# The last expert of a mixture layer taken in halves: gate and up alternating, down in two column halves, and the closing norm split to match

## The reference, cut to what matters

```python
def run_block(args):
    xb, e = args
    h = jax.nn.silu(xb @ w_gate[e]) * (xb @ w_up[e])
    return h @ w_down[e]
...
    h = h + hier_moe(rms_norm_2(h, norm2_gain[l]), ...)
return rms_norm_2(h, final_gain)
```

## Time and profile before

| | us |
|---|---|
| median of 3 runs | 1339.3 (1339.16 to 1340.51) |
| span of the profiled execution, first to last instruction | 1338.3 |
| PE busy / DVE busy / ACT busy | 993.2 / 455.8 / 301.0 |
| 16 DMA engines: data moved, mean rate over the span | 464.39 MB, 347 GB/s |

### The profile page before, as it was taken

One profiled execution on the slowest core, in us unless ns is written; L12 is line 12 of the kernel. 1 busy time (PEld: TensorE's weight loads), 2 busy tenths in 40 slices (PEclk: granted clock), 3 DMA queues, 4 the chain that ended last, 5 costly groups with the idle time before them and its releaser, 6 DMA issues.

```text
span 1338.3 us, 21477 instructions
## 1 busy us (share of the span) xinstructions
PE 993.2 (74%) x9156; PEld 645.0 (48%) x9156; DVE 455.8 (34%) x1013; ACT 301.0 (22%) x644; POOL 41.8 (3%) x38
## 2 busy tenths in 40 slices
PE   9999999999999876566465756756575675657575
PEld 6997778788865443233232323423242342324242
DVE  4697786688854321111110111111011111101111
ACT  5655353647442101001000110100011000101001
POOL 0000201002120000000000000000000000000000
PEclk9999999999999998788787978878797887879787
DMA  9462455325495999999999999999999999999996
GB/s 323 161 248 73 157 189 178 109 95 193 186 417 191 390 429 428 426 429 428 428 429 429 428 428 429 428 429 429 428 428 429 428 428 429 429 428 428 429 427 259
DMA packets 63348, 464.39 MB, mean 347 GB/s; under 512 B 6922, under 2 KB 15940, under 8 KB 38596
## 3 DMA queue, kind: packets, MB, share of 16 engines
q1 hardware_dynamic: 62368, 460.80, 83.6%
q10 hardware_dynamic: 932, 2.92, 0.6%
HBM read 462.66 MB, written 1.05 MB: 346 GB/s over the span
## 4 chain that ended last, share of the span: by engine, by line
DMA 51%; PE 41%; DVE 4%; SPq 2%; issue 1%; ACT 1%; POOL 0%; POOLq 0%; DVEq 0%; ACTq 0%
DMA ring<-in_w_up 50%; PE bank L2156 16%; PE bank L2683 14%; PE bank L2110 3%; PE bank L2134 2%; PE bank L2204 1%; DVE ring_lo L1332 1%; SPq L643 1%; PE bank L2217 1%; DMA consts<-in_consts 1%; PE bank L2700 1%; DVE qk L1303 0%; DVE ring_lo L1337 0%; PE bank L2254 0%; SPq L601 0%
## 5 line engine op out<-in xcount | busy, mean ns | idle before, releaser
L2683 PE MATMUL bank<-ring,expert_area 128*32 128x256 f32 x3840 | 309.8, 493 | 230.5 <-DMA ring<-in_w_up 230.5
L2683 PEld LDWEIGHTS bank<-ring,expert_area 128*32 128x32 f32 x3840 | 146.7, 141 | 387.7 <-DMA ring<-in_w_up 251.2
L1983 DVE TENSOR_TENSOR expert_area<-expert_area,bank 128x128 f32<-128x128 f32 x64 | 24.0, 375 | 476.2 <-ACT expert_area L1224 476.2
L2700 PE MATMUL bank<-ring,consts 128*32 128x256 f32 x1952 | 118.0, 382 | 74.4 <-DVE consts L1986 74.4
L2156 PE MATMUL bank<-ring_lo,xt_hi 128*128 128x512 f32 (+3 forms) x544 | 171.8, 383 | 0.3 <-DVE xt_lo L1533 0.3
L1224 ACT ACTIVATE expert_area<-bank 128x128 f32<-128x128 f32 x64 | 17.7, 277 | 623.3 <-PE bank L2683 623.3
L2700 PEld LDWEIGHTS bank<-ring,consts 128*32 128x32 f32 x1952 | 60.5, 109 | 127.9 <-DVE consts L1986 56.9
L2156 PEld LDWEIGHTS bank<-ring_lo,xt_hi 128*128 128x128 f32 x544 | 99.0, 188 | 18.5 <-issue 1.7
L2156 PE MATMUL bank<-ring_lo,xt_lo 128*128 128x512 f32 (+2 forms) x224 | 84.9, 379 | 0.0
L1990 DVE COPY consts<-bank 32x256 f32<-32x256 f32 x62 | 26.1, 421 | 128.8 <-PE bank L2700 128.8
L2769 PE MATMUL bank<-consts,expert_area 128*128 128x512 f32 x120 | 55.1, 601 | 16.2 <-DVE consts L1991 16.2
(11 more groups left out here) (339 smaller groups left out, 1193.7 us busy)
## 6 DMA issues: line engine op xcount, KB each, us to landing
ring<-in_w_down SPq DMA_DIRECT2D x60, 2048.0 KB, 25.1
ring<-in_w_gate SPq DMA_DIRECT2D x59, 2048.0 KB, 18.4
ring<-in_w_up SPq DMA_DIRECT2D x58, 2048.0 KB, 22.9
ring<-in_moba_w_kv SPq DMA_DIRECT2D x4, 2048.0 KB, 8.2
ring<-in_moba_w_in SPq DMA_DIRECT2D x4, 2048.0 KB, 8.1
ring<-in_w_in SPq DMA_DIRECT2D x3, 2048.0 KB, 7.9
ring<-in_mla_w_uq SPq DMA_DIRECT2D x4, 1152.0 KB, 5.9
ring<-in_mla_w_in SPq DMA_DIRECT2D x8, 512.0 KB, 8.7
```

The lines of the kernel that those rows point to most:

```text
L1983: nc.vector.tensor_tensor(hidden.rearrange("p (k q) -> p k q", k=4), *gate_up, ALU.mult).then_inc(hidden_ready, 1)
L2683: last = nc.tensor.matmul(hidden_in[SLOTS * j:SLOTS * j + SLOTS, :], picked[:, c, SLOTS * i:SLOTS * i + SLOTS], both[:, :, c, j, :], start ...
L2700: last = nc.tensor.matmul(down_in[SLOTS * j:SLOTS * j + SLOTS, :], hidden_t[:, SLOTS * k:SLOTS * k + SLOTS], w[k][:, 256 * j:256 * j + 256 ...
```

## The change

On SP, gate and up of the last expert come as four 1 MB loads: first halves of gate and up, then second halves. Down comes as two halves of columns (512 of 1024, so pieces of 2 KB), not of rows. On PE, gate and up wait for each pair of halves; between the two, ten bf16 matmuls of 512 columns into an idle bank run (`stay_awake(10)`). Down is done for 512 columns (`last_down(0)`), drained, summed into the first half of both tiles (`last_sums(0)`), and then the same for the other 512 columns. A sum of a half has four turns of two matmuls (32 rows x 128 columns), each turn waiting for the one before it.

In the closing norm, the first half's squares (ACT) and products with the gain (DVE) come after `last_sums(0)` and before the drain of the second half. Of the second half, ACT squares tile 0; DVE copies tile 1 out and squares it with a summing product of two operands. One power on POOL serves both tiles. ACT scales the first halves and stores them; DVE finishes the second halves, and SP stores them.

The gain row is loaded as one row of 4 KB; PE spreads it by a matmul with a row of ones (half 0 after expert 60, half 1 after the sum of experts 60 and 61), and DVE copies each half out of the idle bank.

```diff
@@ SP, load_last_expert and the stores
-                sp.dma_start(gate_up[:, 0], src).then_inc(last_landed[0], 16)
-                src = t["w_up_2"][0, e].rearrange("(p c) f -> p c f", c=KD)
                 for half in range(2):
                     at = slice(4 * half, 4 * half + 4)
-                    sp.dma_start(gate_up[:, 1, at], src[:, at]).then_inc(last_landed[half], 16)
+                    for k, name in enumerate(("w_gate_2", "w_up_2")):
+                        src = t[name][0, e].rearrange("(p c) f -> p c f", c=KD)
+                        sp.dma_start(gate_up[:, k, at], src[:, at]).then_inc(last_landed[half], 16)
                 down_taken(e - 1)()
...
                 for half in range(2):
-                    at = slice(2048 * half, 2048 * half + 2048)
-                    sp.dma_start(ring[:, 2, at], src[:, at]).then_inc(last_landed[2 + half], 16)
+                    at = slice(512 * half, 512 * half + 512)
+                    sp.dma_start(dst[:, :, at], src[:, :, at]).then_inc(last_landed[2 + half], 16)
...
+            for tile in range(TILES):
+                sp.wait_ge(out_ready, tile + 1)
+                sp.dma_start(t["out"][0, tile * P:(tile + 1) * P, 512:D], wide[:, tile, 512:D]).then_inc(out_stored, 16)
@@ ACT
-            load_row(final_row, t["final_gain_2"], row_landed)
+            act.dma_start(gain_row, t["final_gain_2"].rearrange("(a n) -> a n", a=1)).then_inc(row_landed, 16)
...
+            act.wait_ge(last_half_in_psum, 1)
+            nc.scalar.copy(last_out[1][0:64, 0:P], last_down_in[0][0:64, :]).then_inc(last_half_act, 1)
+            def first_half_squares(multiplied):
+
+                final_squares(0, 0).then_inc(first_half_squared, 1)
+                act.wait_ge(row_multiplied, multiplied + 1)
+                final_squares(1, 0).then_inc(first_half_squared, 1)
+
+            act.wait_ge(final_in_psum, 1)
+            first_half_squares(0)
+            act.wait_ge(down_in_psum, NE)
+            nc.scalar.copy(last_out[1][0:64, P:2 * P], last_down_in[1][0:64, :]).then_inc(down_drained_act, 1)
...
+            act.wait_ge(final_in_psum, 2)
+            final_squares(0, 1).then_inc(final_squared, 1)
+            n, a, _ = RSQRT["final"]
             act.wait_ge(rsqrt_done, n + 1)
...
+            for tile in range(TILES):
+                nc.scalar.mul(wide[:, tile, 0:512], res[:, tile, 0:512], rstd[:, a + tile:a + tile + 1]).then_inc(
+                    out_ready_act, 1)
+                act.wait_ge(out_ready_act, tile + 1)
+                act.dma_start(t["out"][0, tile * P:(tile + 1) * P, 0:512], wide[:, tile, 0:512]).then_inc(out_stored, 16)
@@ DVE
+            def first_half_multiplied(squared):
+
+                for tile in (1, 0):
+                    if tile == 0:
+                        dve.wait_ge(first_half_squared, squared + 1)
+                    nc.vector.tensor_tensor(res[:, tile, 0:512], final_sum[tile][0][:], final_row[:, 0:512],
+                                            ALU.mult).then_inc(row_multiplied, 1)
+
...
                         drain_down(n, i)
+                        dve.wait_ge(row_in_psum, i + 1)
+                        nc.vector.tensor_copy(final_row[:, 512 * i:512 * i + 512], idle_bank[:]).then_inc(row_ready, 1)
...
+                dve.wait_ge(final_in_psum, 1)
+                dve.wait_ge(row_ready, 2)
+                first_half_multiplied(0)
+                dve.wait_ge(down_in_psum, NE)
+                nc.vector.tensor_copy(last_out[1][64:P, P:2 * P], last_down_in[1][64:P, :]).then_inc(
+                    down_drained_dve, 1)
...
             dve.wait_ge(final_in_psum, 2)
+            link(nc.vector.tensor_copy(last_sum, final_sum[1][1][:]))
+            link(nc.vector.tensor_tensor_reduce(square_dve, last_sum, final_sum[1][1][:], 1.0, 0.0, ALU.mult,
+                                                ALU.add, small[:, 147:148]))
+            dve.wait_ge(final_squared, 1)
+            link(nc.vector.tensor_tensor(small[:, 148:150], small[:, 144:146], small[:, 146:148], ALU.add))
+            ask("final", nc.vector.tensor_scalar(variances("final"), small[:, 148:150], 1 / D, RMS_EPS, ALU.mult,
+                                                 ALU.add))
+            r = rsqrt("final")
+            for tile in range(TILES):
+                nc.vector.scalar_tensor_tensor(wide[:, tile, 512:D], final_sum[tile][1][:], r[:, tile:tile + 1],
+                                               final_row[:, 512:D], ALU.mult, ALU.mult).then_inc(out_ready, 1)
@@ PE
+            def row_broadcast(half):
+
+                nc.tensor.matmul(idle_bank[:], const("ones")[0:1, :], gain_row[:, 512 * half:512 * half + 512],
+                                 start=True, stop=True).then_inc(row_in_psum, 1)
+
+            def stay_awake(n):
+
+                pairs = consts[:, 0:2 * P].bitcast(BF16)
+                for _ in range(n):
+                    nc.tensor.matmul(idle_bank[:], pairs[:, 0:P], pairs, start=True, stop=True)
...
                 last.then_inc(last_back_in_psum, 1)
+                pe.wait_ge(row_landed, 16)
+                row_broadcast(0)
                 expert(n, 1)
...
                 last.then_inc(final_begun, 1)
+                pe.wait_ge(row_ready, 1)
+                row_broadcast(1)
...
+                def last_down(half):
+
+                    pe.wait_ge(last_landed[2 + half], 16)
+                    w = ring[:, 2, :].rearrange("p (k n) -> p k n", k=4)
+                    for k in range(4):
+                        for j in range(4):
+                            at = 512 * half + P * j
+                            last = nc.tensor.matmul(last_down_in[half][SLOTS * j:SLOTS * j + SLOTS, :],
+                                                    hidden_t[:, SLOTS * k:SLOTS * k + SLOTS], w[:, k, at:at + P],
+                                                    start=(k == 0), stop=(k == 3))
+                    last.then_inc((last_half_in_psum, down_in_psum)[half], 1)
+
+                def last_sums(half):
...
+                    for turn in range(4):
+                        pe.wait_ge(final_begun, 3 + 3 * half + turn)
+                        for tile in range(TILES):
+                            j = (turn + 2 * tile) % 4
+                            rows = slice(SLOTS * j, SLOTS * j + SLOTS)
+                            last = nc.tensor.matmul(final_sum[tile][half][:, P * j:P * j + P],
+                                                    last_back[rows, P * (2 + tile):P * (2 + tile) + P],
+                                                    last_out[1][rows, P * half:P * half + P], start=False,
+                                                    stop=(turn == 3), skip_group_check=True)
+                        last.then_inc(final_in_psum if turn == 3 else final_begun, 1)
+
                 expert(n, 2)
-                packed_sums(0)
+                packed_sums()
                 i, x = GROUP - 1, GROUP * n + GROUP - 1
                 for half in range(2):
-                    pe.wait_ge(last_landed[half], 16 * (2 - half))
+                    pe.wait_ge(last_landed[half], 32)
                     gate_and_up(i, ring[:, 3:5, :], range(4 * half, 4 * half + 4))
+                    if half == 0:
+                        stay_awake(10)
                 hidden_turned(x)
                 for half in range(2):
-                    pe.wait_ge(last_landed[2 + half], 16)
-                    down(ring[:, 2, :], (2 * half, 2 * half + 1))
-                packed_sums(1)
+                    last_down(half)
+                    last_sums(half)
```

More of the change, by code:

```diff
@@ L349, in build @@
         final_sum = [[bank[4], bank[5]], [bank[6], bank[7]]]
+        last_down_in = [bank[0][:, 0:P], bank[3][:, 2 * P:3 * P]]
+        gain_row = early_down[0:1, 0:D]
+        last_sum = early_down[:, D:D + 512]
+        square_out = [early_down[:, a:a + 512] for a in (D + 512, 2 * D, 2 * D + 512)]
+        square_dve = early_down[:, 3 * D:3 * D + 512]
+        idle_bank = bank[1]
         hidden_in = bank[2][:, 0:2 * P]
@@ L773, in _ @@
                     load_further_experts(0, ROUNDS - 1, NE * p)
-            for n, (tile, at) in enumerate(((0, 0), (0, 512), (1, 512))):
-                half = slice(at, at + 512)
-                sp.wait_ge(out_ready, n + 1)
-                sp.dma_start(t["out"][0, tile * P:(tile + 1) * P, half], wide[:, tile, half]).then_inc(out_stored, 16)
+            for tile in range(TILES):
+                sp.wait_ge(out_ready, tile + 1)
+                sp.dma_start(t["out"][0, tile * P:(tile + 1) * P, 512:D], wide[:, tile, 512:D]).then_inc(out_stored, 16)
             sp.wait_ge(out_stored, 16 * 4)
@@ L1246, in _, with final_squares @@
                     drain_down(ROUNDS - 1, i)
-                else:
+                elif i == 2:
                     act.wait_ge(down_in_psum, NE - GROUP + i + 1)
-                    nc.scalar.copy(last_out[i - 2][0:64, :], down_in[0:64, :]).then_inc(down_drained_act, 1)
```

(45 more changed lines are left out.)

56 lines of the change are left out of this document (20 added, 36 removed).

## The result

| | us |
|---|---|
| before, median of 20 runs | 1339.56 (1338.54 to 1340.61) |
| after, median of 20 runs | 1342.72 (1340.74 to 1346.60) |
| ratio after/before, 95% interval | 1.0024 [1.0018, 1.0030] |
| profiled execution of after: time, span | 1342.51, 1340.7 |

The change is slower by 3.2 us, a little more than the 2.7 us that a measurement can tell, and half a microsecond outside the range. The runs of after lie in two groups: sixteen from 1340.7 to 1343.6, and four at 1345.05, 1346.08, 1346.58 and 1346.60 (the upper group). In all runs whose span is on record, of after and of the experiments, the time is the span plus 1.75 to 2.04 us, most often 1.8. If that holds for the profiled execution of before too, it took, with its span of 1338.3, about 1340.1 and not 1339.3.

What follows compares the result with a forecast made beforehand. The DMA stream of expert weights and what follows its end bound the kernel. Terms of -3.4 us to hidden complete, +3.7 to the sums' end and -0.5 after gave -0.2: 1339.1 us, range 1336.2 to 1342.2.

Steps and rivals of the forecast that it cites:

- Row: Gain row loaded as 4 KB: shortens the weight stream, so everything after it lands 1.25 us earlier (bounds 0 and 1.27).
- Gate and up: Last expert's alternating halves: second half starts at 1319.25, hidden complete at 1321.2 against 1324.56, a gain of 3.4 us.
- Ten fillers: Matmuls between the halves of gate and up: about 0.21 us each, done at 1318.0, before the second half lands.
- Down's halves: Last expert's down by columns: first half lands at 1322.0 and takes 1.1 us on PE, second half lands at 1324.4.
- Four turns: Sums of each column half: 0.53 us a turn, 2.1 us for four (1.8 to 3.1).
- The clock: PE in the last expert and sums: the sum has it at 2.4 GHz throughout, though a fall keeps a chance.
- the second drain: Drain of down's second half: waits for squares and products, not PE; 2.05 us with these, over at 1327.9.
- a sign that its sum is wrong: At down's second half: the sum is wrong if its drain waits for PE.
- cold rival: Clock falls by the second half of gate and up, slowing products, down and sums: 1342.5 us, chance 0.22.
- The norm: Closing norm and stores after the sums: 7.9 us against 8.4, a gain of 0.5 (0 to 1).
- last term: End of the closing norm: 2.9 us from the last issue's end to the end, as in the kernel before.
- sizes that were called unknown: Turns -0.6 to +2, down's halves -0.3 to +1.7, norm +-0.5: by themselves 1337.7 to 1341.8 us.

Runs made afterwards that it cites:

- E2: E1 plus gate and up in alternating halves and the ten fillers, with down, sums and norm as before: 1338.57 us, ratio 0.9998.
- E1: The kernel before with only the gain row changed to a 4 KB load and its two broadcasts: 1338.06 us, ratio 0.9994.
- E7: E6 with the drain of down's second half moved ahead of the first half's squares and products: 1341.44 us, ratio 1.0017.
- E9: The whole change with twenty fillers between the halves of gate and up in place of ten: 1343.87 us, ratio 1.0035.
- E3: The whole change with more fillers: 4 after the second half's products, 2 after down's first half, 3 after its second: 1341.27 us, ratio 1.0028.
- E4: The whole change without the ten fillers: 1342.77 us, ratio 1.0028.
- E12: The whole change with broadcasts and fillers placed as in E11: 1341.02 us, ratio 1.0015.
- E6: The whole change with fillers over the whole last round, those of E5 and E3 included: 1342.23 us, ratio 1.0022.
- E8: E7 with one set of four turns, four matmuls each, summing both halves behind both drains: 1340.2 us, ratio 1.0009.
- E5: E2 with bf16 fillers in every gap of TensorE in the last round: 1338.48 us, ratio 0.9996.
- E11: E10 with fillers placed anew: 8 ahead of expert 61, 5 ahead of 62, 6 between the halves, 2 to 4 elsewhere: 1338.1 us, ratio 0.9993.
- E10: E2 without fillers and with both broadcasts of the gain row ahead of expert 61: 1338.88 us, ratio 0.9997.

## Why the prediction was wrong, point by point

- **Row:** right. The prediction took 1.25 us; the traces show 1.27 (after, E2) and 0.8 to 1.07 (E1).
- **Gate and up:** right in the profile: second half at 1319.54 (1319.25 forecast), hidden complete, that is all products of gate and up done, at 1321.47 (1321.2). But expert 62's sums end at 1315.4, not 1314.0, since the clock fell while it ran. That ate the lead that was to make the fillers free.
- **Ten fillers:** costed at nothing, covered by the first half's early start. In E7 the cover is gone, and the second half begins 2.3 us late. That the upper group of after is such a mode is worked out and not seen in a profile of after. E9's code is that of after up to the fillers, and in its profile the first half begins at 1319.46 instead of 1315.41, because the clock fell in the sums of experts 60 and 61. With ten fillers the second half would then begin 4.05 us later than in after's profile; added to the usual 1342.7 this makes 1346.8, or, taking ten of the twenty fillers off the 1347.47 of E9, whose sums kept the clock, 1345.3. The group lies from 1345.05 to 1346.60. E7's 1317.7 cannot be carried over, because of its four fillers ahead of the first half. E3, with the same ten, has four runs of nine up there; E4, with no fillers, and E12, with six, have none, and E6, with ten and others in the gaps, has none in eight.
- **Down's halves:** right, 1.08 (1.1), landing at 1321.96 and 1324.52 (1322.0, 1324.4).
- **Four turns:** right at full clock, 2.15 in E3 (2.1).
- **The clock: this is the step that failed.** "The sum has PE at 2.4 GHz throughout." The clock fell in the first sums. The first sums cost 0.4 more than forecast and down's second half 0.84; the second drain waited for PE, 0.47 us, which the prediction had named as a sign that its sum is wrong, so that the second sums began at 1329.0 (1328.15), and they cost 1.3 more. Sums complete at 1332.4 where 1330.25 was forecast: +2.15. The cold rival named the cause and put it in the wrong place: it had the second half of gate and up at 1.2 GHz, which ran at 2.4 in after and, with no filler ahead of it, in E4; that its price, 1342.5, lies near the measured 1342.7 is luck. E3 shows it from the other side: where the clock stays up, down's second half takes 1.08 and the second sums 2.15, and from the hidden complete to the sums complete it is 8.9 us against the 9.05 forecast.
- **The norm:** mis-sized by 0.4 (8.3 against 7.9; 8.5 in E3), nearly all of it in the last term: from the last issue's end to the end it is 3.3 us and not 2.9, because one landing, at 1340.32, comes 0.47 us behind all others. The way to the power is 1.3 us shorter, as meant (1332.4 to 1335.05, 2.65; before 1329.9 to 1333.86, 3.96). Against before it is given back behind the power: ACT scales, issues, scales and issues in one line, so that the last issue ends 2.4 us after it instead of 1.6, and then comes the late landing.
- **The execution that was compared:** the prediction took the profiled execution of before to be a median one, by an offset of 1.0 from span to time. With an offset of 1.8 it was 0.8 above the median of three runs that the prediction went by, and 0.5 above that of the twenty (1339.56). The profiled execution of after is 0.2 below its own median.
- **The range:** the sizes that were called unknown add up, with the forecast of 1339.1, to 1337.7 below but to 1343.3 above (2 + 1.7 + 0.5), not 1341.8. A range up to there would have held the result, but by luck: the turns and down's halves had the sizes forecast for them wherever the clock was up.

In the profile: 1338.1 + 2.15 + 0.4 = 1340.65, measured 1340.7. In the medians: 2.4 between the two spans, and the 0.5 and 0.2, make 3.1, measured 3.2.

The lesson of E2 lies behind these: even the gain that came was not to be had. Everything ends at the landing of down's second half, and the old tail needs 11.5 us from there (1323.67 to 1335.2); the new one needs 14.2 at full clock (1324.09 to 1338.3) and 16.2 as it ran (1324.52 to 1340.7).

## What to carry to other kernels

Ask of each part what bounds the end once it is done: here gate and up came 3 us earlier, and the next thing to be late was the last landing, so the work to cut was what follows that landing, and the split made it longer. A chain of small dependent steps is paid by the hand-over and not by the columns (0.54 against 0.57 for half the matmuls), so splitting it doubles it, and it is also where the clock was lost. A filler is free only while its cover stands: give it the number that fits the worst start, and look at single runs, since a median hides a mode of one run in five.

## What the hardware showed beyond what was expected

- **The clock fell though PE was hardly idle.** In after it was at 2.4 GHz for 17 us, stayed there over idle times of 1.16 us twice, and fell in the first sums, where PE is idle for 0.06 to 0.07 us from turn to turn and the longest idle time of the 2 us before is 0.46. In E7 it fell at 1304.0, after 9 us of which PE was busy for 8.03 (1295 to 1304), 4.7 of them the 64-row sums and the broadcast of one row. The Trainium skill, TensorE: Matmul & The Clock Gate, section "Why this matters for your kernels", ties the drop to longer idle gaps between bursts; there is none in these stretches, and here the measurement decides. What exactly is counted stays open. Of the profiled executions with the new sums, the five with bf16 fillers in the gaps around them (E3, E6, E7, E8, E12) kept the clock through them, and of the three without (after, E4, E9) one did, E9. So the fillers went with a clock that held and are not shown to be its cause; E5 and E7, where it fell under expert 62, show that they don't ensure it.
- **One DMA engine can set the end.** In E11 the sums end 0.6 later than in E2, the span 2.3 later. The DMA views from 1329 us (E11) and 1328 us (E2) give the store that ACT issues 4.7 and 2.7 us from issue to landing:

```profile
out<-wide ACTq DMA_DIRECT2D x1, 256.0 KB, 4.7
```

```profile
out<-wide ACTq DMA_DIRECT2D x1, 256.0 KB, 2.7
```

  E11's rate in the same view, in slices of 0.225 us:

```profile
GB/s 0 0 0 0 0 0 0 0 0 0 0 100 391 373 228 100 464 373 383 373 382 383 410 410 137 27 27 27 27 18 27 27 27 18 0 0 0 0 0 0
```

  Each store counts 16 landings. In E11, 60 of the 64 are in by 1334.97, and the last four follow alone, 0.6 us apart, to 1337.07, while the rate is 27 GB/s, about a sixteenth of the stream's 429: by this, one engine of the sixteen was late. The last landing trails by 0.5 to 0.6 us in after, E3, E6 and E12 and by 1.1 to 1.6 in E7, E9 and E10; in before, E1, E2 and E8 by 0.05 at most. So a part of the scatter, and of the long profiled executions of E7 and E9, lies neither in PE nor in the stream. Why that engine was late is not settled.
